# A two-layer hybrid trunk on one core: first tile scaled behind its transpose, small weights on another queue, two top-k rounds in earlier slots

## What is computed

```
h = rms_norm(x) * norm_g[layer]
u, v, z_a, q, k, v_b, z_b, qi, ki, wi, g_a, g_b = split(h @ w_in[layer])   # 6216 columns
y_a = gelu(u) * (masked_ws @ layer_norm(gelu(v)) + bs) * silu(z_a)
score = sum over 8 heads of wi * relu(qi . ki)        # lightning indexer
keep the 128 largest scores of each query's row, softmax attention over these keys
y_b = attention * silu(z_b)
x = x + (sigmoid(g_a) * (y_a @ w_oa) + sigmoid(g_b) * (y_b @ w_ob)) @ w_out
```

## Time and profile before

| | before |
|---|---|
| median of 3 runs | 788.47 us |
| the profiled execution's own time | 789.69 us |
| its span, first to last instruction | 787.9 us |
| TensorE (matmul) busy | 777.9 us, 99% |
| VectorE busy | 641.4 us, 81% |
| ScalarE busy | 381.6 us, 48% |
| GpSimd busy | 130.3 us, 17% |
| mean granted TensorE clock | 0.998 |

### The profile page before, as it was taken

How to read it: one execution, slowest core, us unless ns; L and a number is a source line. 1 busy time by engine, 2 the same in 40 slices (tenths; PEclk the granted TensorE clock), 3 DMA queues, 4 the chain that set the end, 5 groups by cost and what they waited for, 6 DMA issues and landing times.

```text
span 787.9 us, 11493 instructions
## 1 busy us (share of the span) xinstructions
PE 777.9 (99%) x4124; PEld 669.1 (85%) x4124; DVE 641.4 (81%) x1078; ACT 381.6 (48%) x706; POOL 130.3 (17%) x117
## 2 busy tenths in 40 slices
PE   7999999999999999999999999999999999999998
PEld 7988888888788889988899888888887888899886
DVE  5769999979888767669986799999788887656895
ACT  6566645341344437734664775533324434567242
POOL 1247510000000003012211674000000001120130
PEclk9999999999999999999999999999999999999999
DMA  9635232323231246795873522323232233388584
GB/s 332 221 96 145 82 107 65 97 81 107 80 107 54 66 95 106 191 267 121 186 240 95 174 82 81 107 81 108 68 93 81 82 107 53 81 157 266 139 145 123
DMA packets 44841, 97.89 MB, mean 124 GB/s; under 512 B 3056, under 2 KB 3248, under 8 KB 44784
## 3 DMA queue, kind: packets, MB, share of 16 engines
q1 hardware_dynamic: 32320, 67.12, 27.1%
q0 software_dynamic: 12176, 29.45, 18.2%
q10 hardware_dynamic: 288, 0.59, 0.2%
HBM read 90.85 MB, written 6.29 MB: 123 GB/s over the span
## 4 chain that ended last, share of the span: by engine, by line
PE 86%; DVE 10%; DMA 2%; ACT 1%; issue 1%; DVEq 0%; ACTq 0%; SPq 0%
PE bank L807 17%; PE bank L809 17%; PE bank L808 17%; PE bank L928 5%; PE bank L874 3%; PE bank L876 3%; PE bank L875 3%; PE bank L844 3%; PE bank L845 3%; PE bank L846 3%; PE bank L781 2%; PE bank L799 2%; DVE w_lo L1355 2%; PE bank L737 1%; PE bank L790 1%; DMA x_sb<-in_x 1%
## 5 line engine op out<-in xcount | busy, mean ns | idle before, releaser
L1355 DVE TENSOR_TENSOR w_lo<-w_raw,w_hi 128x1024 fp32r<-128x1024 f32 x144 | 186.7, 1311 | 10.4 <-ACT w_hi L1013 5.6
L1013 ACT ACTIVATE w_hi<-w_raw 128x1024 fp32r<-128x1024 f32 x144 | 148.0, 1054 | 22.2 <-DMA w_raw<-in_w_out 14.6
L807 PE MATMUL bank<-h_lo,w_hi 128*128 128x512 f32 x320 | 128.0, 400 | 0.0
L809 PE MATMUL bank<-h_hi,w_hi 128*128 128x512 f32 x320 | 124.8, 390 | 0.0
L808 PE MATMUL bank<-h_hi,w_lo 128*128 128x512 f32 x320 | 124.6, 389 | 0.0
L807 PE MATMUL bank<-w_lo,h_hi 128*128 128x512 f32 x256 | 100.5, 393 | 0.0
L809 PE MATMUL bank<-w_hi,h_hi 128*128 128x512 f32 x256 | 99.9, 390 | 0.0
L808 PE MATMUL bank<-w_hi,h_lo 128*128 128x512 f32 x256 | 99.9, 390 | 0.0
L686 POOL DMA_DIRECT2D w_raw<-in_w_in x16 | 19.4, 1220 | 408.4 <-DVE w_lo L1355 407.9
L809 PEld LDWEIGHTS bank<-h_hi,w_hi 128*128 128x128 f32 x320 | 60.1, 188 | 12.9
L808 PEld LDWEIGHTS bank<-h_hi,w_lo 128*128 128x128 f32 x320 | 60.2, 188 | 12.3
(11 more groups left out here) (201 smaller groups left out, 1720.6 us busy)
## 6 DMA issues: line engine op xcount, KB each, us to landing
w_raw<-in_w_in SPq DMA_DIRECT2D x92, 512.0 KB, 3.7
w_raw<-in_w_in POOLq DMA_DIRECT2D x16, 512.0 KB, 5.9
w_raw<-in_w_out POOLq DMA_DIRECT2D x16, 512.0 KB, 6.3
w_raw<-in_w_out SPq DMA_DIRECT2D x12, 512.0 KB, 4.2
out<-x_sb POOLq DMA_DIRECT2D x4, 1024.0 KB, 5.9
w_raw<-in_w_oa SPq DMA_DIRECT2D x8, 512.0 KB, 3.2
w_raw<-in_w_ob SPq DMA_DIRECT2D x8, 512.0 KB, 3.9
x_sb<-out POOLq DMA_DIRECT2D x2, 2048.0 KB, 11.5
```

Of the source, the lines that this page charges most:

```text
L807: nc.tensor.matmul(dst, s_h, m_l, start=(n == 0), stop=False)
L809: last = nc.tensor.matmul(dst, s_h, m_h, start=False, stop=(n == len(pairs) - 1))
L1013: nc.scalar.activation(hi, w_raw[:, raw_slot(layer, u)], ACT.Copy).then_inc(s_whi.sem, 1)
L1355: nc.vector.tensor_tensor(lo, w_raw[:, raw_slot(layer, u)], hi.bitcast(F32), ALU.subtract) \
```

## The change

Four parts. (1) For the first tile of layer 0 alone the gain is no longer multiplied in before the transpose: `xn` is written in two halves as x times the reciprocal, TensorE transposes each half as soon as it is there, and the gain, which after the transpose is one number per partition, goes in as ScalarE's `scale` and VectorE's first operand, in eight blocks of 128 columns each. The gain's eight columns come with the identity, in one load (`eye_g`). TensorE waits for each block's remainder. (2) `norm_bc` is issued behind ScalarE's work on tile 0 and is first needed by tile 1; `s_raw` of layer 0 is issued on SP behind unit 1 in place of POOL. (3) `WARM_UP` is 14 in place of 18. (4) Two rounds of `(3, 1)` go from jobs 30 and 31 to jobs 25 and 27, in both layers.

```diff
-WARM_UP = 18
+WARM_UP = 14
...
-              23: [(2, 1), (3, 2)], 26: [(3, 1)], 28: [(3, 2)], 29: [(3, 1)], **{s: [(3, 1)] for s in range(30, 40)}}
+              23: [(2, 1), (3, 2)], 25: [(3, 1)], 26: [(3, 1)], 27: [(3, 1)], 28: [(3, 2)], 29: [(3, 1)], **{s: [(3, 1)] for s in range(32, 40)}}
...
+                    if layer == 0 and u == 2:
+                        sp.dma_start(s_raw[:], w_in[0:1, :, COL["ik"]:COL["ik"] + SMALL]
+                                     .rearrange("a (k p) n -> p (a k) n", p=P)).then_inc(s_small0, 16)
...
-                if layer == 0:
-                    small_weights(0)
...
+                    if first:
+                        pe.wait_ge(s_xnhalf, half + 1)
...
+                        if t == 0 and layer == 0:
+                            pe.wait_ge(s_lo0, k + 1)
...
-            act.dma_start(eye[:], ident).then_inc(s_eye, 16)
-            act.dma_start(norm_bc[:], norm_g[0]).then_inc(s_norm0, 16)
+            act.dma_start(eye_g[:], ident).then_inc(s_eye, 16)
...
+                            nc.scalar.activation(h_hi[:, kk, ORDER[0] * P:(ORDER[0] + 1) * P],
+                                                 bank[1 + kk // 2][:, k % 2 * P:(k % 2 + 1) * P], ACT.Copy,
+                                                 scale=g_col[:, kk:kk + 1]).then_inc(s_hi0, 1)
...
             x_std(0, 0)
+            act.dma_start(norm_bc[:], norm_g[0]).then_inc(s_norm0, 16)
...
+                            dve.wait_ge(s_hi0, kk - kk % 2 + 2)
+                            nc.vector.scalar_tensor_tensor(h_lo[:, kk, tok], bank[1 + kk // 2][:, k % 2 * P:(k % 2 + 1) * P],
+                                                           g_col[:, kk:kk + 1], h_hi[:, kk, tok].bitcast(F32),
+                                                           ALU.mult, ALU.subtract).then_inc(s_lo0, 1)
...
+                for half in range(2):
+                    cols = slice(half * W512, (half + 1) * W512)
+                    nc.vector.tensor_scalar(xn[:, 0, cols], x_sb[:, ORDER[0], cols], rstd[:, c:c + 1], None,
+                                            ALU.mult).then_inc(s_xnhalf, 1)
```

More of the change, by code:

```diff
@@ L316, in trunk @@
         score = sb("score", [P, sum(P * (b + 1) for b in range(1, TILES))])
-        eye = sb("eye", [P, P])
+        eye_g = sb("eye_g", [P, P + KD])
+        eye, g_col = eye_g[:, 0:P], eye_g[:, P:P + KD]
         rope = sb("rope", [P, TILES, DH + ID])
@@ L353, in trunk @@
         s_x0 = [ctx.enter_context(nc.semaphore(f"x_in{t}")) for t in range(TILES)]
+        s_small0 = ctx.enter_context(nc.semaphore("first_small_weights_in"))
         s_small_in = sig("small_weights_in", 16, False)
@@ L437, in trunk @@
         s_stash2 = sig("x_stashed_tiles_23", 16, False)
+        s_xnhalf = ctx.enter_context(nc.semaphore("first_tile_half_normalised"))
+        s_hi0 = ctx.enter_context(nc.semaphore("first_tile_hi_written"))
+        s_lo0 = ctx.enter_context(nc.semaphore("first_tile_lo_written"))
         s_eye = ctx.enter_context(nc.semaphore("identity_in"))
@@ L713, in transpose_x @@
             def transpose_x(layer, t):
-                pe.wait_ge(s_xn.sem, s_xn.at(layer, t + 1))
+                first = layer == 0 and t == 0
+                if not first:
+                    pe.wait_ge(s_xn.sem, s_xn.at(layer, t + 1))
                 if t >= 2:
@@ L718, in transpose_x @@
                 for half in range(2):
-                    dst = bank[3 + 2 * (t % 2) + half]
+                    if first:
+                        pe.wait_ge(s_xnhalf, half + 1)
                     for k in range(4):
                         kk = 4 * half + k
-                        last = nc.tensor.transpose(dst[:, k * P:(k + 1) * P], xn[:, t % 2, kk * P:(kk + 1) * P], eye[:])
+                        if first:
+                            dst, col = bank[1 + kk // 2], k % 2 * P
+                        else:
+                            dst, col = bank[3 + 2 * (t % 2) + half], k * P
+                        last = nc.tensor.transpose(dst[:, col:col + P], xn[:, t % 2, kk * P:(kk + 1) * P], eye)
                     last.then_inc(s_xt.sem, 1)
@@ L736, in transpose_rotated @@
                 for c in range(0 if index and ORDER[n] == 0 else 4):
-                    last = nc.tensor.transpose(bank[5][:, c * P:(c + 1) * P], rot[:, c * P:(c + 1) * P], eye[:])
+                    last = nc.tensor.transpose(bank[5][:, c * P:(c + 1) * P], rot[:, c * P:(c + 1) * P], eye)
                 if index:
-                    last = nc.tensor.transpose(bank[6][:, 0:P], rot[:, IH * ID:IH * ID + 2 * ID], eye[:])
+                    last = nc.tensor.transpose(bank[6][:, 0:P], rot[:, IH * ID:IH * ID + 2 * ID], eye)
                 last.then_inc(s_rott.sem, 1)
@@ L757, in transpose_ws @@
                 for g in range(A_GROUPS):
-                    last = nc.tensor.transpose(bank[5][:, g * P:(g + 1) * P], ws_raw[:, g], eye[:])
+                    last = nc.tensor.transpose(bank[5][:, g * P:(g + 1) * P], ws_raw[:, g], eye)
                 last.then_inc(s_wst.sem, 1)
@@ L790, in attend @@
                         last = nc.tensor.transpose(bank[5][:, c * P:(c + 1) * P],
-                                                   probs[:, (i - 1) % 2, c * P:(c + 1) * P], eye[:])
+                                                   probs[:, (i - 1) % 2, c * P:(c + 1) * P], eye)
                     last.then_inc(s_pt.sem, 1)
@@ L943, in index_job @@
                     for k in ks:
-                        if k % (KD // 2) == 0:
+                        if t == 0 and layer == 0:
+                            pe.wait_ge(s_lo0, k + 1)
+                        elif k % (KD // 2) == 0:
                             pe.wait_ge(s_hlo.sem, s_hlo.at(layer, 2 * t + k // (KD // 2) + 1))
@@ L1283, in h_rounded @@
                     act.wait_ge(s_xt.sem, s_xt.at(layer, 2 * t + half + 1))
+                    if layer == 0 and t == 0:
+                        act.wait_ge(s_eye, 16)
+                        for k in range(4):
+                            kk = 4 * half + k
+                            nc.scalar.activation(h_hi[:, kk, ORDER[0] * P:(ORDER[0] + 1) * P],
+                                                 bank[1 + kk // 2][:, k % 2 * P:(k % 2 + 1) * P], ACT.Copy,
+                                                 scale=g_col[:, kk:kk + 1]).then_inc(s_hi0, 1)
+                        act.wait_ge(s_hi0, 4 * half + 4)
+                        act.sem_inc(s_hhi.sem, 1)
+                        continue
                     nc.scalar.activation(h_hi[:, 4 * half:4 * half + 4, ORDER[t] * P:(ORDER[t] + 1) * P],
@@ L1288, in small_rounded @@
             def small_rounded(layer):
-                act.wait_ge(s_small_in.sem, s_small_in.at(layer, 16))
+                if layer == 0:
+                    act.wait_ge(s_small0, 16)
+                else:
+                    act.wait_ge(s_small_in.sem, s_small_in.at(layer - 1, 16))
                 act.wait_ge(s_job.sem, slot_free(layer, 0))
@@ L1673, in h_remainder @@
                 for half in halves:
+                    if layer == 0 and t == 0:
+                        dve.wait_ge(s_eye, 16)
+                        for k in range(4):
+                            kk, tok = 4 * half + k, slice(ORDER[0] * P, (ORDER[0] + 1) * P)
+                            dve.wait_ge(s_hi0, kk - kk % 2 + 2)
+                            nc.vector.scalar_tensor_tensor(h_lo[:, kk, tok], bank[1 + kk // 2][:, k % 2 * P:(k % 2 + 1) * P],
+                                                           g_col[:, kk:kk + 1], h_hi[:, kk, tok].bitcast(F32),
+                                                           ALU.mult, ALU.subtract).then_inc(s_lo0, 1)
+                        dve.wait_ge(s_lo0, 4 * half + 4)
+                        dve.sem_inc(s_hlo.sem, 1)
+                        continue
                     dve.wait_ge(s_hhi.sem, s_hhi.at(layer, 2 * t + half + 1))
@@ L1683, in first_tile @@
             def first_tile(layer):
-                dve.wait_ge(s_norm if layer else s_norm0, 16)
-                x_normalised(layer, 0)
+                if layer:
+                    dve.wait_ge(s_norm, 16)
+                    x_normalised(layer, 0)
+                    return
+                c = 2 * TILES * HEADS
+                dve.wait_ge(s_xstd.sem, s_xstd.at(0, 1))
+                vec.link(dve, nc.vector.reciprocal(rstd[:, c:c + 1], std[:, c:c + 1]))
+                for half in range(2):
+                    cols = slice(half * W512, (half + 1) * W512)
+                    nc.vector.tensor_scalar(xn[:, 0, cols], x_sb[:, ORDER[0], cols], rstd[:, c:c + 1], None,
+                                            ALU.mult).then_inc(s_xnhalf, 1)
+                dve.wait_ge(s_xnhalf, 2)
+                dve.sem_inc(s_xn.sem, 1)
             def small_remainder(layer):
@@ L1700, in _ @@
                 if layer == 0:
+                    dve.wait_ge(s_norm0, 16)
                     x_normalised(layer, 1)
@@ L1777 @@
```

(3 more changed lines are left out.)

## The result

The changed kernel takes **799.04 us** in the median of six runs (797.88 to 801.56), beside 788.42 us (788.12 to 790.87) for the kernel before on the same chip. The ratio is 1.014, with a 95% interval of 1.0128 to 1.0151: slower, 2.0 us above the predicted 797.0 and just above the range's upper end.

What follows compares the result with a forecast made beforehand. TensorE, busy 99% of the span, was taken as the bound, with VectorE deciding in stretches. Head 0, rounds +6.1 and clock +2.4 us make +8.5 us on the 788.47 us median: 797.0 us, range 794.0 to 799.0.

Steps and rivals of the forecast that it cites:

- The mechanism of the rounds: Two rounds ahead of the gates of jobs 25 and 27 delay the first attention division 3.04 us per layer: +6.1 us.
- VectorE has the room: Rival: VectorE's 2.66 us of idle pieces absorb the rounds, each stand grows only 0.4 us; 787 to 789 us, chance 0.05.
- the clock's term: TensorE's clock falls after each lengthened wait for `probs`, costing 1.2 us per layer: +2.4 us.
- one such stretch, whole: Upper bound of the clock's extra cost per stand: 1.64 us, from the head's half-clock stretch at 25.00 to 28.40 us.
- clock holds: Rival: stands grow by 3.04 us but TensorE's clock stays up through both; 794.6 us, chance 0.22.
- The head at 0 us: The head's earlier start gains nothing, as x's last tile lands no sooner: 0 us.
- the head gives something: Rival: the earlier start is worth 1 to 2 us after all; 795 to 796 us, chance 0.10.
- near 10: Sign in the head: TensorE's first index product starts near 10 us.
- the very line that I had drawn: Sign of a wrong forecast: x's last tile lands more than half a microsecond away from 20.2 us.
- The small rows are dear: Rival: `s_raw` on SP's queue holds up x's tiles by 1 to 4.7 us; 798 to 802 us, chance 0.10.
- the wait ahead of tile 2's products: Sign in the head: TensorE waits there longer than 1.0 us, and these products start near 25 us as before.
- one low stretch behind each stand: Sign: one stretch at clock 0.50 follows TensorE's 3.7 us wait for `probs` in both layers.

Runs made afterwards that it cites:

- filled stands: 14 products that nothing reads ahead of TensorE's wait for the first `probs` per layer: with the rounds alone moved 794.99 us, with the whole change 795.55 us.
- the one with 7 products: The changed kernel plus 7 products that nothing reads ahead of TensorE's wait for the first `probs` of each layer: 797.74 us.
- two near versions: The changed head alone, rounds as before: with `s_raw` back on GpSimd's queue 789.29 us, with the warm-up back at 18 788.79 us.

## Why the prediction was right and wrong

**The mechanism of the rounds held.** They stood inside VectorE's unbroken chain, each stand grew by 3.02 us for a predicted 3.04, and no gap gave anything back. The runs back the reason: one round gives half of the stand's growth, and the same two rounds in job 24's wait cost nothing. With that the rival "VectorE has the room" falls: its 2.66 us of idle pieces were no room. I had read them a little wrong: the longest is 0.32 us, not 0.2, and the 0.6 us for the exponential stands at 211.4, outside that stretch.

**The step that failed is the size of the clock's term**, "2 x 1.2 = +2.4 us" with "one such stretch, whole" as its upper bound. It measured 3.5 to 4.0 us between unfilled and filled stands, and 4.2 and 4.0 us by the products of two single executions. That a stand would cost clock was right, only its size was off. The bound itself was wrong: I took the head's low stretch of 3.4 us for the longest there is, but after the same stand of 3.7 us the records show 3.4 us once and 6.8 us the other time, in both profiled kernels. The long one cost 2.8 us where it lay almost whole behind the stand, and 2.4 us where 1.7 us of it fell into the stand, both well over my 1.64; the short ones cost 1.35 and 1.6 us. That a part can fall into the stand, which I had counted, is so; that a stretch can be twice as long I had not. The six runs, from 797.9 to 801.6 us at mean clocks of 0.996 to 0.989, scatter in part by this: the two slowest have the lowest clock. The Trainium skill (TensorE: Matmul & The Clock Gate, on why this matters for your kernels) has idle gaps between bursts send the clock back to its half rate. The rows agree with that for stands of 3.7 us, four times out of four; a stand of 2.2 us kept the clock twice in one profile and lost it twice in another, the one with 7 products.

With the measured sizes the sum closes, as far as terms taken from neighbours of the same kernel can show that: 788.4 + 6.1 + 4.0 = 798.5, and 0 to 0.7 us for the head makes 798.5 to 799.2. Measured: 799.04.

**The rival "clock holds"** is refuted as it stands, but the filled kernels are that case made by hand. Their 795.0 and 795.6 us answer to its 794.6.

**The head at 0 us** held, or nearly: +0.7 us with an interval that begins at +0.1, and in two near versions +0.8 and 0.0 us with intervals that hold zero. The rival "the head gives something" falls. The first index product came "near 10". x's last tile landed at 19.68, half a microsecond from 20.2 and so on the very line that I had drawn; the five profiles with the old head spread from 19.56 to 20.41, so the line was too narrow to tell anything. "The small rows are dear" falls by the kernel with `s_raw` back on GpSimd's queue. Two details were wrong. I had the wait ahead of tile 2's products longer than 1.0 us; in the changed kernel it is absent, since TensorE reaches that place late through the new waits on `index_lo` and `xn`, 2.5 us together, which I had not seen. In the four profiles with this head whose first index product starts at 9.1 to 9.7 us, a wait of 0.6 to 0.8 us stands there again. And I had one low stretch behind each stand, but did not say what happens to the one at 25 us, which was absent. That it was gone is not a merit of the head: in the profile with the head alone a low stretch of 3.4 us came at 12.3 us instead.

```profile
12.30:15.70 3.40, 3.31 (x14) 2.95 (x13) 3.14 (x8) 2.07 (x4) 0.00 (x0) 0.50 1.02 343
```

Nor does a low stretch stand at 25 us as a rule in the kernel before: 41 of its 65 runs beside the experiments have a mean clock of 1.0.

**What stays open.** Why the low clock lasts twice as long after one stand as after the other, and why 2.2 us of idle time kept the clock up in one profile and not in the other. What makes the times of one kernel scatter at an equal mean clock, and why one run of the head with the old warm-up shows a mean clock of 0.947 at only 791.27 us. Whether the new head costs anything: 787.31 against 786.78 us and 789.31 against 788.58 point to half a microsecond. By the medians only the version with the old warm-up has no loss (788.79 for 788.78), but the intervals don't part them. The new head loses clock more often: a mean clock of 0.998 or less stands in 39 of the 57 runs of the five kernels that have it and whose stands did not grow, and in 18 of 72 with the old head. That this costs time is not shown: with the head alone the runs at 0.998 took 789.0 to 790.3 us, those at 1.0 788.7 to 790.3.

## What to carry to other kernels

Before you move work forward on an engine that works in order, follow the chain back to the last place where that engine waited for another. In this kernel work put into that wait was free up to its length, and work behind it arrived in full at the far end, 26 to 37 us later. Here one to three jobs' distance parted 10 us from nothing, and the move that paid was the one out of the chain into that gap. Where a move lets TensorE stand for microseconds, count the stand, and then the clock behind it as a range, since it differs from one execution to the next: here each stand of 3.7 us cost 1.35 to 2.8 us of clock besides itself.

## What the runs showed of the hardware

- After two stands of 3.7 us in one program the granted clock was 0.50 for 3.4 us and for 6.8 us, in either order. By the products behind them this cost 1.35 and 2.8 us in one profile, 1.6 and 2.4 us in the other.
- Two stands of 2.2 us left the clock at 1.00 in one profile (790.89 us, mean clock 0.999); in another two idle times of 2.2 us, each behind seven products that nothing reads, were followed by 0.50 for 3.4 us each. Other runs of the first kernel had mean clocks of 0.995 to 0.997 and took 792.7 to 796.1 us.
- Fourteen products that nothing reads, put into each stand, kept the clock up (0.997 to 1.0 in all eleven runs of two kernels) and made them 4.0 and 3.5 us faster without a change to what it waits for.
- 1,024 rows of 288 bytes took 6.3 to 6.6 us from issue to landing on SP's queue (seven profiles) and 7.5 to 7.8 us on GpSimd's (six profiles). GpSimd issued them 0.7 us sooner, so they landed at 8.4 to 8.7 and at 8.9 to 9.2 us.
